# Banded attention with stationary keys and a 65th row for the shift; rough products of the context unit spread; row gathers asked for two experts ahead

## What is computed

```python
def swa_latent(q, k, v, k_ctx, v_ctx, sink):      # 6 heads of 64, 2 key heads, window 128
    def block(i, q_b):                            # 128 queries
        valid = (abs(q_pos[:, None] - k_pos[None, :]) <= 128) & inside
        s_loc = where(valid, einsum('bqgrd,bkgd->bgrqk', q_b, k_b) * SWA_SCALE, -inf)
        s_ctx = einsum('bqgrd,bcgd->bgrqc', q_b, k_ctx) * SWA_SCALE
        p = softmax(concat([s_ctx, s_loc, sink]))[..., :-1]
        return p[ctx] @ v_ctx + p[band] @ v_b
def swa_context(q, k, v, sink):                   # 256 queries on 256 keys, layer 0 only
    return softmax(concat([q @ k * SWA_SCALE, sink]))[..., :-1] @ v
def mla_block(qn, qr, kn, kr, v):                 # 6 heads of 64 + 32, all 1280 keys
    return softmax((qn @ kn + qr @ kr) * MLA_SCALE) @ v
def ec_ffn(h, router_w, w_gate, w_up, w_down):    # each of 16 experts picks its tokens
    xg = h[idx]                                   # 128 latent rows, 32 context rows
    y = (silu(xg @ w_gate) * (xg @ w_up)) @ w_down * top_aff
    return zeros.at[idx].add(y)
```

## Time and profile before

| what | value |
|---|---|
| runs | 4520.48, 4528.03, 4524.14 us; median 4524.14 |
| profiled execution, own time | 4528.48 us |
| its span | 4526.7 us, mean granted clock 0.933 |
| PE busy | 4064.9 us (90%) x20694 |
| DVE, ACT, POOL busy | 2177.9 (48%), 1305.5 (29%), 516.6 us (11%) |
| transfers | 453.30 MB, 100 GB/s |

### The profile page before, as it was taken

How to read it: one execution, slowest core, us unless ns; L and a number is a source line. 1 busy time by engine, 2 the same in 40 slices (tenths; PEclk the granted TensorE clock), 3 DMA queues, 4 the chain that set the end, 5 groups by cost and what they waited for, 6 DMA issues and landing times. The chain is left out here.

```text
span 4526.7 us, 51891 instructions
## 1 busy us (share of the span) xinstructions
PE 4064.9 (90%) x20694; PEld 3154.7 (70%) x20694; DVE 2177.9 (48%) x3350; ACT 1305.5 (29%) x2261; POOL 516.6 (11%) x600
## 2 busy tenths in 40 slices
PE   7989899896999969898988699799976999998997
PEld 5878655573777758885656599677744778886875
DVE  3567655523111145776552433465566365553344
ACT  3234533313111122344332233321354211111232
POOL 1000211102122120002110111110102100000012
PEclk8989999997999979998999899899988999999999
DMA  6100000237767641000011799412001211112111
GB/s 246 33 15 1 16 1 1 102 146 320 258 235 257 213 150 58 19 1 16 1 61 39 299 342 341 131 42 89 21 1 47 81 46 47 47 47 77 49 56 56
DMA packets 73878, 453.30 MB, mean 100 GB/s; under 512 B 8000, under 2 KB 12624, under 8 KB 57680
## 3 DMA queue, kind: packets, MB, share of 16 engines
q1 hardware_dynamic: 56960, 389.73, 22.9%
q0 software_dynamic: 13088, 47.19, 3.8%
q10 hardware_dynamic: 3632, 13.63, 0.7%
HBM read 394.95 MB, written 55.57 MB: 100 GB/s over the span
## 5 line engine op out<-in xcount | busy, mean ns | idle before, releaser
L2313 PEld LDWEIGHTS psum<-words,words 128*128 128x128 f32 x4096 | 515.0, 192 | 10.4 <-issue 7.9
L2313 PE MATMUL psum<-words,words 128*128 128x160 f32 (+1 forms) x4096 | 516.3, 288 | 1.4 <-DVE words L435 0.9
L718 PE MATMUL psum<-words,words 128*128 128x512 f32 x1104 | 443.5, 402 | 27.4 <-DVE words L758 22.9
L720 PE MATMUL psum<-words,words 128*128 128x512 f32 x1104 | 439.2, 398 | 0.0
L719 PE MATMUL psum<-words,words 128*128 128x512 f32 x1104 | 439.0, 398 | 0.0
L1641 PE MATMUL psum<-words,words 128*128 128x428 f32 (+1 forms) x720 | 253.9, 353 | 22.8 <-DVE words L1734 22.8
L718 PEld LDWEIGHTS psum<-words,words 128*128 128x128 f32 x1104 | 210.1, 190 | 80.2 <-DVE words L758 24.6
L1353 PE MATMUL psum<-words 128*128 128x512 f32 (+1 forms) x504 | 263.9, 606 | 0.0
L1642 PE MATMUL psum<-words,words 128*128 128x428 f32 (+1 forms) x720 | 250.5, 348 | 0.0
L1425 DVE TENSOR_REDUCE words<-psum 128x1 f32<-128x512 f32 (+1 forms) x300 | 162.3, 586 | 183.1 <-PE psum L1323 182.5
L1643 PE MATMUL psum<-words,words 128*128 128x428 f32 (+1 forms) x720 | 249.8, 347 | 0.0
(11 more groups left out here) (437 smaller groups left out, 8038.6 us busy)
## 6 DMA issues: line engine op xcount, KB each, us to landing
words<-in_w_gate SPq DMA_DIRECT2D x32, 2048.0 KB, 8.0
words<-in_w_up SPq DMA_DIRECT2D x32, 2048.0 KB, 12.5
words<-in_w_down SPq DMA_DIRECT2D x32, 2048.0 KB, 12.4
words<-in_ada_w SPq DMA_DIRECT2D x24, 2048.0 KB, 14.9
words<-in_w_in SPq DMA_DIRECT2D x55, 512.0 KB, 3.5
words<-in_w_up SPq DMA_DIRECT2D x44, 512.0 KB, 3.4
words<-in_w_down SPq DMA_DIRECT2D x44, 256.0 KB, 2.6
words<-in_x SPq DMA_DIRECT2D x2, 5120.0 KB, 23.2
```

What stands on the lines that cost most here:

```text
L718: pe.matmul(out, hi[:, j, w], S.parts[0](kt, t0, nt), start=(kt == 0), stop=False)
L720: mm = pe.matmul(out, lo[:, j, w], S.parts[0](kt, t0, nt), start=False, stop=(kt == KD - 1))
L2313: mm = pe.matmul(k.bank[m % 2][:, u * W:(u + 1) * W], ring[:, j, w0:w0 + P], xgT[:, j, kt, 0:W], start=(kt == 0), stop=(kt == KD - 1))
```

## The change

Three parts. **Window attention** is written anew after the pattern of latent attention. Per head there are 14 steps in layer 0 (12 in layer 1), each with one stationary key tile and 256 to 512 moving queries: two exact passes, one on 128 rows and one on 65 (`klo` with a row of ones, `q1` with the shift in row 64), and a mask for band tiles. Maxima now come from rough products of the high parts (64 rows), one tile of queries at a time at one place in PSUM, for the next head; the shift goes through `shift_rows` and ScalarE's `row`, which also makes the sink's row; GpSimd makes the low part of the queries. The output of 256 or 512 columns is divided in halves of 256. **Latent attention**: the context unit has no rough products; the second latent unit makes those of the context unit and of the first latent unit after it, the buffers of maxima are three instead of two. **Experts**: two gathers stand ahead of the loop, and in it gather(e+2) takes the place of gather(e+1).

```diff
 def window_attention(k, l, with_ctx):
...
+    parts = ([(0, NCTX, 2)] if with_ctx else []) + [(NCTX, 512, 0), (NCTX + 512, 512, 1)]
...
+    ctx_steps = lambda g: [(t, parts[g][0], parts[g][1], None) for t in range(CT)]
...
+    body = [st for g in range(lat + 1) for st in ctx_steps(g)]
+    body += [band_step(b) for b in range(3)] + ctx_steps(lat + 1) + [band_step(b) for b in range(3, NB)]
+    L = len(body)
+    N = H * L
...
+    NP = tiles_of[NG]
+    skip = (2, 4) if L - NP > 3 else (2,)
+    piece_step = [i for i in range(L) if i not in skip][:NP]
+    shift_step = [min(piece_step[tiles_of[g + 1] - 1] + 1, L - 1) for g in range(NG)]
...
+
+    outs = []
+    for h in range(H):
+        for g in range(NG):
+            for x in range(parts[g][1] // 256):
+                outs.append((h * L + closes[g] + LAG + 0.5 + x, h, g, x))
+    outs.sort()
...
+            def rough(h, p):
+                g, t0 = query_tile[p]
+                n = h * NP + p
+                if p == 0:
+                    pe.wait_ge(q1_set, h + 1)
+                if n:
...
+                q = q1[0:64, h % 3, t0:t0 + P]
+                S = k.psum[:, S_COL:S_COL + NCTX]
+                mm = pe.matmul(S, q, keys[0:64, h % 2, 0:NCTX], start=True, stop=True)
...
+                    lo, hi = max(b - 1, 0), min(b + 2, NB)
+                    B = k.bank[1]
+                    pe.matmul(B[:, 0:(hi - lo) * P], q, keys[0:64, h % 2, NCTX + lo * P:NCTX + hi * P], start=True, stop=False, skip_group_check=True)
+                    mm = pe.matmul(B[:, 0:(hi - lo) * P], idb, masked(b), start=False, stop=True, skip_group_check=True)
+                mm.then_inc(a_full, 1)
...
+            def shift_rows(h, g):
+                G = h * NG + g
+                pe.wait_ge(m_set, G + 1)
+                if G:
+                    pe.wait_ge(m_row, G)
...
+            def exact(x):
...
+                for g in range(NG):
+                    if opens[g] == x % L:
+                        pe.wait_ge(m_row, h * NG + g + 1)
+                if x >= 2:
+                    pe.wait_ge(p_set, x - 1)
+                C, key = k.bank[C_BANK[x % 2]], slice(t * P, (t + 1) * P)
+                pe.matmul(C[:, 0:n], keys[:, h % 2, key], q2[:, h % 2, q0:q0 + n], start=True, stop=False, skip_group_check=True)
+                mm = pe.matmul(C[:, 0:n], klo[0:ROW + 1, h % 2, key], q1[0:ROW + 1, h % 3, q0:q0 + n], start=False, stop=hide is None, skip_group_check=True)
+                if hide is not None:
+                    mm = pe.matmul(C[:, 0:n], idb, hide, start=False, stop=True, skip_group_check=True)
+                mm.then_inc(c_full, 1)
...
+            def values(x):
+                h, st = x // L, body[x % L]
+                for g, (t0, n, bank) in enumerate(parts):
+                    if opens[g] == x % L:
+                        if h:
+                            pe.wait_ge(o_out, o_count[h - 1, g])
+                        pe.wait_ge(e_set, h * NG + g + 1)
+                        pe.matmul(k.bank[O_BANK[bank]][:, 0:n], to_den[SROW:SROW + 1, :], es[SROW:SROW + 1, h % 3, t0:t0 + n],
+                                  start=True, stop=False, skip_group_check=True)
...
+                for g, c0, n, b0 in segments(st):
+                    mm = pe.matmul(k.bank[O_BANK[parts[g][2]]][:, b0:b0 + n], SV[:, 2 * st[0] + h % 2, :], pt[:, x % R, c0:c0 + n],
...
+            pe.wait_ge(k_hi, 4)
+            pe.wait_ge(mask_set, 3)
+            for p in range(NP):
+                rough(0, p)
+            for g in range(NG):
+                shift_rows(0, g)
+            pe.wait_ge(k_lo, 2)
+            pe.wait_ge(ones_set, 2)
+            pe.wait_ge(sink_set, 1)
+            for x in range(N):
+                h, i = x // L, x % L
+                exact(x)
+                if h + 1 < H:
+                    if i in piece_step:
+                        rough(h + 1, piece_step.index(i))
+                    for g in range(NG):
+                        if shift_step[g] == i:
+                            shift_rows(h + 1, g)
+                if x >= LAG:
+                    values(x - LAG)
+            for x in range(N - LAG, N):
+                values(x)
...
+            def row(h, g):
+                G, (t0, n, _) = h * NG + g, parts[g]
+                act.wait_ge(m_full, G + 1)
+                act.activation(q1[ROW:ROW + 1, h % 3, t0:t0 + n], k.bank[M_BANK][ROW:ROW + 1, 0:n], ACT.Copy).then_inc(m_row, 1)
+                act.wait_ge(m_row, G + 1)
+                act.activation(es[SROW:SROW + 1, h % 3, t0:t0 + n], q1[ROW:ROW + 1, h % 3, t0:t0 + n].bitcast(F32), ACT.Exp,
+                               bias=sink[ROW:ROW + 1, h:h + 1], scale=SWA_SCALE).then_inc(e_set, 1)
...
+            for x in range(N):
+                h, i = x // L, x % L
+                act.wait_ge(c_full, x + 1)
+                if x >= R:
+                    act.wait_ge(d_done, x - R + 1)
+                n = body[i][2]
+                act.activation(pt[:, x % R, 0:n], k.bank[C_BANK[x % 2]][:, 0:n], ACT.Exp, scale=SWA_SCALE).then_inc(p_set, 1)
+                if h + 1 < H:
+                    for g in range(NG):
+                        if shift_step[g] == i:
+                            row(h + 1, g)
+                    if i == 1:
+                        high_second(h + 1)
+                    if i == 3 and h + 2 < H:
+                        high_first(h + 2)
...
+        @block.gpsimd
+        def _(pool):
+            for h in range(1, H):
+                pool.wait_ge(q2_hi, h + 1)
+                pool.tensor_tensor(q2[half(1 - h % 2), h % 2, first:NT], PR[half(h % 2), SQ + h // 2, first:NT],
+                                   q2[half(h % 2), h % 2, first:NT].bitcast(F32), ALU.subtract).then_inc(q2_lo, 1)
...
+            def maximum(h, p):
...
+                dve.wait_ge(a_full, h * NP + p + 1)
+                dve.reduce_max(mx[:, h % 2, p:p + 1], k.psum[:, S_COL:S_COL + NCTX + band_tiles * P], AX.X).then_inc(a_max, 1)
+                if p + 1 == tiles_of[g + 1]:
...
+                    dve.wait_ge(a_max, h * NP + p + 1)
+                    dve.tensor_scalar(nm[:, h % 2, cut], mx[:, h % 2, cut], floor[:, h:h + 1], -1.0, ALU.max, ALU.mult).then_inc(m_set, 1)
...
+                dve.wait_ge(d_done, h * L + closes[g] + 1)
+                if n:
+                    dve.wait_ge(o_out, n)
+                dve.reciprocal(rec[0:64, c], O[64:P, c]).then_inc(r_set, 1)
+                dve.wait_ge(r_set, n + 1)
+                dve.tensor_tensor(MIX[half(h % 2), 3 + h // 2, t0 + c.start:t0 + c.stop], O[0:64, c], rec[0:64, c], ALU.mult).then_inc(o_out, 1)
...
+            for p in range(NP):
+                maximum(0, p)
+            for g in range(2):
+                dve.wait_ge(k_hi, 2 * g + 2)
+                dve.tensor_tensor(klo[0:64, g, :], PR[half(g), SK, :], keys[half(g), g, :].bitcast(F32), ALU.subtract).then_inc(k_lo, 1)
+            dve.wait_ge(q2_hi, 1)
+            dve.tensor_tensor(q2[half(1), 0, first:NT], PR[half(0), SQ, first:NT], q2[half(0), 0, first:NT].bitcast(F32),
+                              ALU.subtract).then_inc(q2_lo, 1)
+            due = [((h - 1) * L + piece_step[p], 0, h, p) for h in range(1, H) for p in range(NP)]
+            due += [(when, 1, n, 0) for n, (when, _, _, _) in enumerate(outs)]
+            for _, kind, a, b in sorted(due):
+                if kind == 0:
+                    maximum(a, b)
+                else:
+                    outputs(a)
...
-    pm, mx = k.at(o + (R + 1) * 512, 2, 4, 4), k.at(o + (R + 1) * 512 + 32, 2, 4)
-    one = k.at(o + (R + 1) * 512 + 48, NT)
+    pm, mx = k.at(o + (R + 1) * 512, 3, 4, 4), k.at(o + (R + 1) * 512 + 48, 3, 4)
...
+    def ahead(u):
+
+        if units[u][3] <= CT:
+            return range(u + 1, u + 1)
+        return range(u + 1, min(u + 2 if u + 1 < N and units[u + 1][3] > CT else u + 3, N))
+
     def share(u, t):
-
-        if u + 1 == N:
+        mine = ahead(u)
+        if not mine:
             return range(0)
-        total, last = upto[u + 2] - upto[u + 1], max(units[u][3] - 2, 1)
-        cut = lambda x: upto[u + 1] + min(total, -(-total * min(x, last) // last))
+        lo, hi, last = upto[mine[0]], upto[mine[-1] + 1], units[u][3] - 2
+        cut = lambda x: lo + min(hi - lo, -(-(hi - lo) * min(x, last) // last))
         return range(cut(t), cut(t + 1))
+    opening = 2 if with_ctx else 1
     first_of = [min(u for u in range(N) if units[u][0] == h) for h in range(H)]
 
...
-            for p in range(upto[1]):
+            for p in range(upto[opening]):
                 rough(p)
...
+                if p == upto[u] and u >= 3:
+                    dve.wait_ge(m_full, u - 2)
+                dve.reduce_max(pm[:, u % 3, q, c0 // 512:c0 // 512 + 1], k.bank[S_BANK[p % 3]][:, 0:n], AX.X).then_inc(a_max, 1)
...
-            for p in range(upto[1]):
+            for p in range(upto[opening]):
                 maximum(p)
...
                 left = [0, 1] if u else []
```

(16 more changed lines are left out.)

260 lines of the change are left out of this document (86 added, 174 removed).

## The result

The changed kernel takes 4580.5 us, median of 4 runs (4576.8 to 4582.2), against 4522.3 of the kernel before in 4 runs (4518.3 to 4528.0): a ratio of 1.013, 95% interval 1.012 to 1.014. It is **slower by 58 us**; the forecast was 4508.

| stage | before | after | difference | forecast |
|---|---|---|---|---|
| window attention, layer 0 | 207.7 | 273.3 | +65.6 | +12.9 |
| window attention, layer 1 | 182.2 | 212.0 | +29.8 | +5.4 |
| latent attention, layer 0 | 310.6 | 276.2 | -34.4 | -26.6 |
| latent attention, layer 1 | 247.3 | 247.0 | 0 | 0 |
| experts, layer 0 | 515.1 | 514.7 | 0 | 0 |

A forecast was written before the change was run, and what follows sets the result against it. TensorE was taken as the bound in window attention. Window attention +18, latent attention -26.6 and experts -7 sum to -16 us, from the median 4524.14 to 4508; range 4496 to 4518, outer range 4482 to 4535.

The forecast's parts named there:

- start: Window attention, before steady work: copies, one-by-one rough pieces and low parts take 31 us in layer 0, 28 in layer 1.
- work of six heads: Window attention, TensorE: 28.0 us per head in layer 0, 158.6 in all; 24.2 per head in layer 1, 137.6.
- waits at head changes: Window attention: TensorE waits for VectorE's maximum, in layer 0 also for the negation; 18.5 us, layer 1 10.5.
- clock: Window attention: granted clock falls at half the ten head changes and after the start, 8 us layer 0, 7 layer 1.
- tail: Window attention's end: the last output halves add 4.5 us in each layer.
- Rival 2: Window attention: clock falls at every head change, 1.7 us each, waits a quarter longer; 4524 us, no change; chance 0.14.
- rival 3: Window attention: the 65-row pass exposes its weight load, 0.19 us per change, 59 us; 4557 us, slower; chance 0.06.
- the second, 1.3 us by GpSimd: Window attention, layer 0: GpSimd's low query half delays VectorE's negation, so shift rows wait 1.3 us more per head change.
- Latent attention: Layer 0: moving rough products out of the context unit brings heads to 44.4 us and saves 26.6 us; layer 1 unchanged.
- Rival 5: Latent attention, layer 0: the second latent unit stalls, 3.3 us return in each of five heads; 4524 us; chance 0.08.
- Experts: Gathers asked two experts ahead remove layer 1's 13 later waits, 7.0 us; each layer's first wait stays; bounds 0 and 7.
- Rivals 3 and 4: Slower, window attention: 3, 65-row passes expose weight load, 4557, chance 0.06; 4, costlier start and doubled waits, 4543, chance 0.06.

## Why the prediction was wrong

Layer 0's window stage is 273.3 us where 220.6 was forecast. Term by term, the heads' work from the version with the outputs later (28.17 us per head at full clock):

| term | forecast | measured |
|---|---|---|
| start | 31 | 31.1 |
| work of six heads | 158.6 | 161.0 (5 x 28.17 and 20.1 for the last) |
| waits at head changes | 18.5 | 9.5 (four of 2.3 to 2.4) |
| clock | 8 | 64.6 (the five spans from head to head, 37.6, 44.3, 44.4, 44.3 and 44.4, less work and waits) |
| tail | 4.5 | 7.1 |

**The term that failed is the clock**, 8 and 7 us in the sum, at 1.7 us a fall. The place was right, and so was the cause of the fall. The price was carried over from a stretch with other work: there passes of 96 and 97 rows run, and the clock was back after 3.4 us. Here each of the four falls cost 13.8 us in layer 0 (177.4 us for four heads, less 4 x 28.17 and 9.5) and 4.0 in layer 1 (125.6 less 4 x 25.35 and 8.2); the start's own stretch cost 9.4 and 4.9 more, and the wait in layer 1's last head 2.6 with its stretch. So the clock took 64.6 us where 8 were forecast, and about 21 where 7 were. Rival 2, the one on the clock, had the right cause at 1.7 us a change, an eighth of what it was in layer 0.

The other steps, in the prediction's order:
- **The work of a head** was right in layer 0, 28.0 for 28.17, and 1.1 us short in layer 1, 24.2 for 25.3. (6 x 24.2 less 7.8 is 137.4, not 137.6; nothing hangs on it.) One step of exact passes, with its mask, shows the prices:

```profile
362.91 0.74 PE L1075 MATMUL psum<-words,words 128*128 128x384 f32 x1
363.49 0.34 PE L1076 MATMUL psum<-words,words 65*128 65x384 f32 x1
363.67 0.34 PE L1078 MATMUL psum<-words,bmask 128*128 128x384 bf16 x1
363.94 0.38 PE L1045 MATMUL psum<-words,words 64*128 64x256 f32 x1
364.16 0.28 PE L1050 MATMUL psum<-words,words 64*128 64x256 f32 x1
```

  The 65-row pass is followed after 0.18 us, the bare price of 384 columns, and the step to 64 rows costs 0.09 more, where the prediction has 0.19 from the earlier trace rows. (The 0.58 us ahead of it hold 0.40 of the f32 product before, whose two parts start at 362.46 and 362.89: from 362.46 to 363.49 are 1.03 us, 0.85 for that product's 512 columns and 0.18 for the pass.) So rival 3 is out: no weight load shows at the passes of 65 rows. The rough products on 64 rows do cost more: the next one follows 256 columns after 0.22 us, where the pass on 65 rows has 0.12. Whether that is a load no run shows. The rule of the Trainium skill, page "TensorE: Matmul & The Clock Gate", section "Part 3: Packing small matmuls", that a load overlaps only where row groups differ, does not hold for the 65-row passes; the same section also has a load go ahead into a background buffer, which would allow what is measured.
- **The waits**: 2.4 and 2.1 us as forecast, but four in a layer where five were counted; the second, 1.3 us by GpSimd, is absent here and came out at 0.9 in the version with the wait filled, where the clock was up.
- **The start** was right at 31 and 28 us (31.1 and 28.1), but the clock was low for 20 us beyond it, up to 351 us. The prediction counted the lower level for the pieces alone.
- **The tail** took 7.1 us for 4.5.
- **Latent attention**: 34.4 us for 26.6. The heads' starts, to be read against the earlier trace rows:

```profile
672.35 0.60 PE L1393 MATMUL psum<-ident,words 128*1 128x128 f32 x4
...
846.46 0.38 PE L1393 MATMUL psum<-ident,words 128*1 128x128 f32 x2
```

  The four heads between these rows by stretch, before and after:

```profile
606.29:807.56 201.27, 186.45 (x625) 110.36 (x624) 109.52 (x172) 66.31 (x108) 22.98 (x8) 0.92 0.00 1
672.35:846.46 174.11, 167.72 (x625) 102.72 (x625) 103.19 (x172) 65.84 (x108) 23.20 (x8) 1.00 0.00 1
```

  Four heads take 174.1 us, 43.5 each, where 44.4 was forecast, the last head 6.9 us less than before (6 forecast), and the first head's 2.9 us for its successor's pieces didn't show. Rival 5 is out. (201.3 less 4 x 44.4 is 23.7, not 23.5; the four heads gave 27.2.) The gain has a part that the prediction doesn't name. Before, the clock fell again and again within these heads (mean 0.92, is one of the falls); now it is up throughout, and TensorE is busy 18.7 us less with the same 625 matmuls, and idle 8.4 us less. An estimate from the clock's shares, 0.08 x 201.3 us, makes up to 16 of the 27.2 us the clock's. No run parts it from the waits that are gone.
- **Experts**: the gather waits went as forecast, the time didn't. The step that failed is "The 13 later waits of layer 1 go, 21.8 - 14.8 = 7.0 us": it costed a wait by its length and didn't ask what is late next. VectorE was, by nearly as much (9.3 us for 2.5). The stage got 2.5 us shorter.

Rivals 3 and 4, the two that ended slower (4557 and 4543), had the wrong mechanisms: no weight load showed at the 65-row passes, and neither the start nor the waits were longer than forecast.

## What to carry to other kernels

A short wait on TensorE can have two prices: its own length, and the stretch at 1.2 GHz behind it. Here the second went from 3.4 to 30.7 us with what ran after the wait, so it must be read from a stretch with the same work, not from another stage. Take the waits out of new work before you judge it: here moving output halves in VectorE's order was worth 95 us, and filling the waits with unused products 66. Where a stage has a start at the lower level, that is the next thing to shorten (22 us here). Where a wait goes away, look for the engine that is late next before the whole wait is booked as gain.

## What the runs showed of the hardware

- In layer 0 the granted clock stayed at 0.50 for 30.7 us after a wait of 2.3 to 2.4 us when the second exact pass had 65 or 66 rows, with TensorE busy 29.89 of 30 us, and for 6.8 to 13.7 us when it had 72, 80 or 96. The spacings at either level were the same (for 384 columns 0.18 us at full clock and 0.32 at the lower level, with 65 and with 96 rows). In layer 1, with 65 rows as well, it stayed for 3.4 to 13.7 us. So TensorE was busy in these 30 us and the clock did not come back. The Trainium skill, page "TensorE: Matmul & The Clock Gate", section "HAM oscillation — how this bites in real kernels", tells of a kernel whose clock falls again at every wait for a transfer, waits longer than these. The falls at every head change agree with it; stretches as long as 30.7 us are not in it.
- The extra rows held only zeros, and shortened the stretches all the same.
- Which waits were followed by a fall: in the changed window attention, behind its start, all eight of 2.0 to 2.4 us and the one of 1.25 us, and in the old form all nine of 2.8 to 3.1 us; in the version with the wait filled, one of the four of 0.9 to 1.0 us in layer 0. In latent attention after the change, from 639 us on, the clock did not fall, with waits of up to 1.6 us.
- With ten unused products in their place (2.5 us at full clock) no wait of 2 us was left at the second rough piece, and the clock stayed up there at all eight places where the change had one.
